# The gates of mixer 2 as rows: their weights become a stationary operand of 128 columns

## The reference, cut to what matters

```python
h = modulate(rms_norm_2(x, norm1_w), shift1, scale1)
p = h @ w_in                      # ..., last 16 columns are the gates
gates = p[..., o5:] + b_gates
...
gt = gates.astype(jnp.float32).reshape(B, S, 4, H).transpose(2, 0, 3, 1)
i_f, f_f, i_b, f_b = gt[0], gt[1], gt[2], gt[3]     # 4 kinds x 4 heads x 256 tokens
h_fwd = mlstm_chunkwise(q, k, v, i_f, f_f)
h_bwd = jnp.flip(mlstm_chunkwise(jnp.flip(q, 2), ..., jnp.flip(i_b, 2), jnp.flip(f_b, 2)), 2)
```

## Time and profile before

| | us |
|---|---|
| median of 3 runs | 2646.25 |
| lowest and highest of the 3 | 2640.28 and 2648.36 |
| the profiled execution, its own time | 2651.8 |
| its span in the profile | 2650.0 |
| PE busy | 2554.6 (96%) |
| DVE busy | 1435.3 (54%) |
| ACT busy | 1127.0 (43%) |
| POOL busy | 1222.3 (46%) |

### The profile page before, as it was taken

How to read it: one execution, slowest core, us unless ns; L and a number is a source line. 1 busy time by engine, 2 the same in 40 slices (tenths; PEclk the granted TensorE clock), 3 DMA queues, 4 the chain that set the end, 5 groups by cost and what they waited for, 6 DMA issues and landing times.

```text
span 2650.0 us, 48874 instructions
## 1 busy us (share of the span) xinstructions
PE 2554.6 (96%) x19040; PEld 2342.0 (88%) x19040; DVE 1435.3 (54%) x2359; ACT 1127.0 (43%) x1320; POOL 1222.3 (46%) x500
## 2 busy tenths in 40 slices
PE   7999999999899999999999999999999999999998
PEld 5887888889899999998888887789899999998886
DVE  3535242636667777776666434436566575444333
ACT  2252222443444444444444334443444444444443
POOL 2663333567444444444444364547344444444442
PEclk9999999999899999999999799999999999999999
DMA  9963343569577777776776464459566656555653
GB/s 397 391 243 127 132 187 156 226 241 347 210 275 271 267 266 269 269 272 249 286 261 258 142 270 158 153 198 344 192 222 219 245 214 222 183 189 176 196 186 125
DMA packets 140376, 611.85 MB, mean 231 GB/s; under 512 B 15584, under 2 KB 15968, under 8 KB 115680
## 3 DMA queue, kind: packets, MB, share of 16 engines
q1 hardware_dynamic: 140256, 610.14, 62.9%
HBM read 607.98 MB, written 2.10 MB: 230 GB/s over the span
## 4 chain that ended last, share of the span: by engine, by line
issue 46%; PE 31%; POOL 20%; DMA 1%; DVE 1%; POOLq 1%; ACT 0%; DVEq 0%; SPq 0%; ACTq 0%
PE psum L1905 31%; POOL wlo L1714 20%; DMA raw<-wstream 1%; DMA ada_raw<-adastream 0%; DVE xT L2227 0%; POOLq L1711 0%; POOLq L1713 0%; PE psum L2121 0%; ACT whi L1725 0%; DVE psum L2227 0%; DVE gslo L2219 0%; ACT arena L1728 0%; ACT gshi L1725 0%; DVE arena L2321 0%; POOLq L1714 0%
## 5 line engine op out<-in xcount | busy, mean ns | idle before, releaser
L1714 POOL TENSOR_TENSOR wlo<-raw,whi 128x1024 fp32r<-128x1024 f32 x496 | 1222.1, 2469 | 1398.9 <-ACT whi L1725 1398.4
L1905 PE MATMUL psum<-hi_h,whi 128*128 128x256 f32 x4224 | 1211.8, 287 | 15.0 <-issue 8.6
L1725 ACT ACTIVATE whi<-raw 128x1024 fp32r<-128x1024 f32 x760 | 800.6, 1059 | 998.2 <-PE psum L1905 785.9
L1905 PE MATMUL psum<-hi_h,wlo 128*128 128x256 f32 x4224 | 1196.6, 283 | 0.0
L1905 PE MATMUL psum<-lo_h,whi 128*128 128x256 f32 x4224 | 1196.0, 283 | 0.0
L1905 PEld LDWEIGHTS psum<-hi_h,whi 128*128 128x128 f32 x4224 | 805.4, 191 | 24.7 <-issue 13.9
L1905 PEld LDWEIGHTS psum<-hi_h,wlo 128*128 128x128 f32 x4224 | 805.3, 191 | 1.9 <-issue 1.7
L1905 PEld LDWEIGHTS psum<-lo_h,whi 128*128 128x128 f32 x4224 | 804.7, 191 | 0.0
L2219 DVE TENSOR_TENSOR wlo<-raw,whi 128x1024 fp32r<-128x1024 f32 x264 | 379.6, 1442 | 277.6 <-ACT whi L1725 277.6
L2227 DVE SCALAR_TENSOR_TENSOR psum<-ada_raw,cact,psum 128x256 f32<-128x256 f32 x702 | 287.5, 481 | 13.2 <-DMA ada_raw<-adastream 13.2
L1905 PE MATMUL psum<-whi,gshi 128*128 128x512 f32 x704 | 277.4, 394 | 4.0 <-DVE gslo L2219 3.5
(11 more groups left out here) (164 smaller groups left out, 1738.6 us busy)
## 6 DMA issues: line engine op xcount, KB each, us to landing
raw<-wstream SPq DMA_DIRECT2D x760, 512.0 KB, 4.6
ada_raw<-adastream SPq DMA_DIRECT2D x168, 1024.0 KB, 7.0
arena<-adastream SPq DMA_DIRECT2D x24, 1024.0 KB, 17.9
xT<-x_in SPq DMA_DIRECT2D x8, 512.0 KB, 7.0
y_out<-xT SPq DMA_DIRECT2D x4, 512.0 KB, 2.6
gs_pages<-tabs_in SPq DMA_DIRECT2D x2, 512.0 KB, 4.4
gs_pages<-rw_in SPq DMA_DIRECT2D x2, 512.0 KB, 7.8
tabs<-tabs_in SPq DMA_DIRECT2D x1, 738.0 KB, 9.5
```

What stands on the lines that cost most here:

```text
L1714: nc.gpsimd.tensor_tensor(wlo[:, q, :], raw[:, q, :], whi[:, q, :].bitcast(F32), ALU.subtract).then_inc(sem.lo_ready, 1)
L1725: return nc.scalar.activation(out_, in_, ACT.Copy, scale=scale)
L1905: return nc.tensor.matmul(o, lhsT, rhs, start=start, stop=stop, skip_group_check=True)
```

## The change

The 16 gate columns of each tile are spread over 128 columns, in groups of four at columns 0, 32, 64 and 96, with zeros between; the new buffer `wgs` (pages 4 to 7 of `arena`, free at that time) holds their high and low parts, 2 x 16 x 128 elements for each partition. DVE clears the whole buffer once (`wz0`), ACT writes the high parts and DVE the low parts into the groups. PE then takes the spread weights as the stationary operand and h as the moving one: 16 products of three matmuls with 256 columns, 48 matmuls in the place of 96. The gates come out as rows: input gates on partitions 0 to 63, forget gates on 64 to 127. The biases become one column for each partition, `gate_bias`, made by DVE with the identity. One matmul with a 64 x 64 identity moves the forget rows to partitions 0 to 63, in place of four. On DVE and ACT the operations on the gates now work on 256 elements in place of 16 or 32, and the two subtractions of `row_c` read the input gates from SBUF, where they read PSUM before. In ACT's program the copy of the gate weights waits for `wz0`; the call `ahead(0, 0)` ahead of it issues nothing new. The three clears of 256 elements become two and the one of 4096.

```diff
--- before.py
+++ after.py
@@ -363,6 +363,7 @@
         self.wg_hi = new("wg_hi")
         self.wg_ready = new("wg_ready")
         self.wz = new("wz")
+        self.wz0 = new("wz0")
         self.x_landed = new("x_landed")
         self.x_made = new("x_made")
         self.x_ready = new("x_ready")
@@ -419,7 +420,9 @@
         gain2, _ = sb("gain2", [P, 16])
         pc, _ = sb("pc", [P, 16])
         xT, _ = sb("xT", [P, KT, S])
-        arena, _ = sb("arena", [P, 15, 1024])
+        arena, arena_at = sb("arena", [P, 15, 1024])
+
+        wgs, _ = sb("wgs", [P, 2, KT, P], F32R, offset=arena_at + 4 * 4096)
         gT = arena[:, 0:11, :].rearrange("p a (b s) -> p (a b) s", s=S)
         gsf, _ = sb("gs_pages", [P, 4, 1024], F32, offset=gs_at)
 
@@ -1160,12 +1163,17 @@
 
             return 9 + ORDER2.index(name) + 1
 
-        wg_hi, wg_lo = gslo[:, 0, 0, :], gslo[:, 0, 1, :]
+
+        def gate_columns(part):
+            return wgs[:, part].rearrange("p k (g r) -> p k g r", r=32)[:, :, :, 0:4]
+
+        wg_in4 = small[:].rearrange("p (k g h) -> p k g h", g=4, h=4)
         dft = halves(19)
-        gate_tok = page(22)[:, 0:256].rearrange("p (k b c) -> p k b c", k=2, b=2)
-        gate_in = page(22)[:, 512:544].rearrange("p (b c) -> p b c", c=16)
-        f_min = page(22)[:, 544:560].rearrange("p (b c) -> p b c", c=8)
-        f_abs = page(22)[:, 560:576].rearrange("p (b c) -> p b c", c=8)
+        gate_bias = stat[:, 6:7]
+        gate_one = page(22)[:, 768:784]
+        FORGET = slice(64, 128)
+        gate_in = page(22)[:, 0:256]
+        f_min, f_abs = page(22)[FORGET, 256:512], page(22)[FORGET, 512:768]
         row_c, row_m, row_b, row_s = (tiles(14)[:, k, :] for k in range(4))
         FWD, BWD, BOTH = slice(0, 32), slice(32, 64), slice(0, 64)
         ccol = pc[:].rearrange("p (b r) -> p b r", r=8)
@@ -1179,7 +1187,7 @@
         hsq, hrms = page(13)[:, 0:512], page(13)[:, 512:768]
         mask_f, mask_b = page(20)[:, S:2 * S], page(20)[:, 0:S]
 
-        def pe_mix2(pe, st, mm, part, spot):
+        def pe_mix2(pe, st, mm, product, part, spot):
             def slot(g, s):
 
                 part(B2 + g * GS, g % 2, 2 * s, 2 * s + 2, "tok" if ORDER2[g][0] in "vu" else None,
@@ -1276,26 +1284,15 @@
                 slot(0, s)
 
             pe.wait_ge(sem.wg_ready, 1)
-            for tb in range(2):
-                o = bank[5][:, tb * 16:(tb + 1) * 16]
-                t = slice(tb * P, (tb + 1) * P)
-                for kt in range(KT):
-                    w = slice(kt * 16, kt * 16 + 16)
-                    mm(o, hhi[:, kt, t], wg_hi[:, w], tb == 0 and kt == 0, False)
-                    mm(o, hlo[:, kt, t], wg_hi[:, w], False, False)
-                    ins = mm(o, hhi[:, kt, t], wg_lo[:, w], False, kt == KT - 1)
-                    if tb and kt == KT - 1:
-                        ins.then_inc(sem.gates, 1)
+            for kt in range(KT):
+                ins = product(bank[5][:, 0:S], wgs[:, 0, kt, :], wgs[:, 1, kt, :], hhi[:, kt, :], hlo[:, kt, :],
+                              kt == 0, kt == KT - 1)
+            ins.then_inc(sem.gates, 1)
             slot(1, 0)
             slot(1, 1)
 
             pe.wait_ge(sem.gt_ready, 1)
-            for k in range(2):
-                for tb in range(2):
-                    ins = mm(bank[4][BOTH, k * S + tb * P:k * S + (tb + 1) * P], gate_tok[:, k, tb, :], ident,
-                       k == 0 and tb == 0, True)
-                    if k and tb:
-                        ins.then_inc(sem.rows_made, 1)
+            mm(bank[4][BOTH, 0:S], ident[FORGET, FORGET], f_min, True).then_inc(sem.rows_made, 1)
             slot(1, 2)
             slot(1, 3)
             slot(2, 0)
@@ -1383,9 +1380,11 @@
                 act.wait_ge(sem.dft_done, 3 * n + 3)
                 copy(halves(MF[n // 2])[:, n % 2, :], bank[6]).then_inc(sem.dft_out, 1)
 
+            ahead(0, 0)
             act.wait_ge(sem.tables2_landed, 48)
-            copy(wg_hi, small[:]).then_inc(sem.wg_hi, 1)
-            for s in range(4):
+            act.wait_ge(sem.wz0, 1)
+            copy(gate_columns(0), wg_in4).then_inc(sem.wg_hi, 1)
+            for s in range(1, 4):
                 ahead(0, s)
             kept("q")
             ahead(1, 0)
@@ -1447,31 +1446,33 @@
 
         def dve_mix2(dve, at, st, tt, ts, stt, unit_rows, scaled):
             V = nc.vector
-            dve.wait_ge(sem.wg_hi, 1)
-            tt(wg_lo, small[:], wg_hi.bitcast(F32), ALU.subtract).then_inc(*at.up(sem.wg_ready))
-            V.memset(page(22)[:, 0:256], 0.0).then_inc(*at.up(sem.step))
             V.memset(page(21)[:, 512:768], 1.0).then_inc(*at.up(sem.step))
             V.memset(page(21)[:, 768:1024], 0.0).then_inc(*at.up(sem.step))
+            dve.wait_ge(sem.slab_used, B2)
+            V.memset(wgs[:].bitcast(F32), 0.0).then_inc(*at.up(sem.wz0))
+            zeroed = at.last
+            tt(gate_one.rearrange("p (g h) -> p g h", h=4), ident.rearrange("p (g r) -> p g r", r=32)[:, :, 0:4],
+               col("bgates", 0, 16).rearrange("p (g h) -> p g h", h=4), ALU.mult).then_inc(*at.up(sem.step))
+            dve.wait_ge(*at.last)
+            V.tensor_reduce(gate_bias, gate_one, AX_X, ALU.add).then_inc(*at.up(sem.step))
+            dve.wait_ge(*zeroed)
+            dve.wait_ge(sem.wg_hi, 1)
+            tt(gate_columns(1), wg_in4, gate_columns(0).bitcast(F32), ALU.subtract).then_inc(*at.up(sem.wg_ready))
             unit_rows()
             one, zero = page(21)[BOTH, 512:768], page(21)[FWD, 768:1024]
 
             dve.wait_ge(sem.gates, 1)
-            tt(gate_in, bank[5][:, 0:32].rearrange("p (b c) -> p b c", c=16),
-               col("bgates", 0, 16).unsqueeze(1).broadcast_to([P, 2, 16]), ALU.add).then_inc(*at.up(sem.step))
-            dve.wait_ge(*at.last)
-            ts(f_min, gate_in[:, :, 8:16], 0.0, None, ALU.min).then_inc(*at.up(sem.step))
-            V.tensor_copy(gate_tok[:, 0].rearrange("p b (d x) -> p b d x", d=2)[:, :, :, 0:4],
-                               gate_in[:, :, 0:8].rearrange("p b (d x) -> p b d x", d=2)).then_inc(*at.up(sem.step))
-            dve.wait_ge(*at.last)
-            stt(f_abs, f_min, 2.0, gate_in[:, :, 8:16], ALU.mult, ALU.subtract).then_inc(*at.up(sem.f_abs))
+            ts(gate_in, bank[5][:, 0:S], gate_bias, None, ALU.add).then_inc(*at.up(sem.step))
+            dve.wait_ge(*at.last)
+            ts(f_min, gate_in[FORGET], 0.0, None, ALU.min).then_inc(*at.up(sem.step))
+            dve.wait_ge(*at.last)
+            stt(f_abs, f_min, 2.0, gate_in[FORGET], ALU.mult, ALU.subtract).then_inc(*at.up(sem.f_abs))
             dve.wait_ge(sem.f_ln, 1)
-            tt(gate_tok[:, 1].rearrange("p b (d x) -> p b d x", d=2)[:, :, :, 0:4],
-               f_min.rearrange("p b (d x) -> p b d x", d=2), f_abs.rearrange("p b (d x) -> p b d x", d=2),
-               ALU.subtract).then_inc(*at.up(sem.gt_ready))
+            tt(f_min, f_min, f_abs, ALU.subtract).then_inc(*at.up(sem.gt_ready))
             unit_rows()
 
             dve.wait_ge(sem.rows_made, 1)
-            gi, gf = bank[4][:, 0:S], bank[4][:, S:2 * S]
+            gi, gf = gate_in, bank[4][:, 0:S]
             V.tensor_tensor_scan(row_b[BOTH], one, gf[BOTH], 0.0, ALU.mult, ALU.add).then_inc(*at.up(sem.step))
             dve.wait_ge(*at.last)
             tt(row_b[BWD], row_b[BWD], gf[BWD], ALU.subtract).then_inc(*at.up(sem.step))
@@ -2203,7 +2204,7 @@
             down(B1_DOWN, 0, 2, 4, True)
             st["free"] = {0: (sem.x_ready, 8), 1: (sem.x_ready, 8)}
             st.update(unit=MIX_UNITS2[0], units=MIX_UNITS2, spots=SPOTS2, slabs=0, after_taken={MIX_UNITS2[0]: 10})
-            pe_mix2(pe, st, mm, part, spot)
+            pe_mix2(pe, st, mm, product, part, spot)
             output(B2_OUT, MIX2, 4, 12, (sem.mix_split, 4, 2))
             up(B2_UP, 1, 24, [(8, 1), (3, 0)])
             down(B2_DOWN, 1, 5, 16, False)
```

## The result

The changed kernel takes 2628.65 us (median of 5 runs, 2623.95 to 2629.92), the kernel before 2643.34 us in the same comparison (5 runs). The ratio is 0.9941 with a 95% interval of 0.9928 to 0.9955: 15.6 us less, between 11.9 and 19.0. The forecast was 13.3 us less, 2633.0 us.

The account below looks back on a forecast made before the run. PE was taken as the bound, busy 2554.6 of 2650.0 us. The terms 11.0 + 1.8 + 0.5 = 13.3 us, taken from the median 2646.25 us, gave 2633.0 us, range 2627 to 2640.

Parts of the forecast that it names:

- The product: Gate product on PE: 48 matmuls of 256 columns at 0.120 us replace 96 of 16 columns, 11.0 us less.
- Rival E: Gate product: PE's time goes by moving columns, so the new product costs 5.0 us more, 2651.3 us; chance 0.01.
- The slab behind it: Slab after the gate product: clock doesn't fall, so its first 20 matmuls take 2.4 us, not 4.2; 1.8 us less.
- Rival B: Gate product and slab behind: the clock falls all the same, only 7.1 us less, 2639.2 us; chance 0.02.
- The turn: Turn of gates to rows on PE: one matmul in place of four, 0.5 us less.
- The weights: Gate weights behind DVE's long clear: ready at 1498.5 to 1499.4, before PE comes at 1499.92; cost 0 us.
- rival A: Before the gate product: POOL holds up DVE's clear and subtraction, weights late, PE stands 3.3 us, 2636.3 us; chance 0.10.
- What was queued behind ACT's wait: High parts of slabs 9 to 11 and SP's slabs 13 to 15 come later, but before PE wants them; cost 0.
- the gates' chain: DVE and ACT operations on the gates grow to 256 elements, done at 1513.6 before PE's turn at 1519.2; cost 0.
- the stream: SP's load of modulation weights waits for PE's spot at the end of slab 11, so everything behind moves with PE.
- Rival C: Behind the spot: transfers are the limit, PE comes earlier only to wait, time about 2646 us; chance 0.05.
- Rival D: DVE's clear of 4096 elements takes 26.8 us, PE stands 21.7 us, 2657.5 us, longer than before; chance 0.02.

Follow-up runs that it names:

- the wide product: The kernel before, each of its 96 gate matmuls moving 128 columns (spread weights) in place of 16, h stationary as before: 2636.19 us, ratio 0.9982.
- the doubled products: Gate product computed twice over, in the kernel before (2665.42 us, ratio 1.0082) and in the changed kernel (2635.84 us, ratio 0.9967).
- clear_twice: The changed kernel with DVE's clear of 4096 elements done twice: 2633.97 us, ratio 0.9964.
- before_again: The kernel before, measured once more with no edit: 2643.70 us against 2643.06 us, ratio 1.0002.
- before_twice: The kernel before with its gate product computed twice over (192 matmuls of 16 columns): 2665.42 us, ratio 1.0082.

## Why the prediction was right, and where it was off

**The product, 11.0 us.** Right: 16.78 to 5.80 us, 10.98 us. That the count of matmuls and not their moving columns sets the time is shown by 0.109, 0.111 and 0.120 us for 16, 128 and 256 columns. Rival E, the time by moving columns, is refuted by the wide product. By the figures of "TensorE: Matmul & The Clock Gate", section "Back-to-back issue gap", of the Trainium skill, the 96 narrow matmuls would have taken 2.4 us; but that section gives them for an isolated matmul, and has it that in a stream of weight loads and matmuls both set the spacing, which the prediction left out. The same page of the Trainium skill has the price that held, in "LDWEIGHTS (loading the stationary operand)": the number of columns divided by 1.2, in ns, so 107 ns for 128. The trace agrees, with 109 ns. That the weight load is what takes this time rests on this agreement: no run multiplied twice with the same weights.

**The slab behind it, 1.8 us.** Right: 1.91 us. Its reason, that the narrow matmuls bring the clock down, was an inference from one place in one trace; the wide and the doubled products bear it out. Rival B didn't occur in any of the seven profiles that have 256 columns and no long standstill.

**The turn, 0.5 us.** Right: 0.45 us.

**The weights, 0 us with a margin of 0.5 to 1.4 us.** Half right, and the one step that failed: that DVE is free for this part at a fixed time. Two things were off. First, the clear of 4096 elements was sized 3.5 us, by the slope between two rows. It takes 4.27 us, if the idle time that stands ahead of each long clear is counted with it, 0.80 us here and 0.2 us ahead of the clear of 1024 elements (0.9 + 0.2 = 1.1 us, again 1.04 to 1.07 ns an element). I take this idle time as the start of the clear, which the row leaves out. The second clear of clear_twice, which ends 4.4 us after the first, fits that. My other end, sixteen times the short one, was the nearer one, and with it the margin was right: 0.7 us where DVE was free in time. "VectorE: DVE Perf Modes", section "Zero memsets can be issued as uint32 (trn2)", of the Trainium skill has a clear at one cycle for each element, which at the 0.96 GHz of that page is 4.27 us, an estimate; the measured 4.27 us agree. The 0.3 us from ACT's copy to DVE's subtraction were misread too, without harm: DVE's operation before had begun only at 1493.26, and in the changed kernel the subtraction began 0.1 us after the copy. Second, I took DVE's start of this part as fixed (1493.27 in a trace where PE came at 1499.92). It isn't: when the last two subtractions of the norm each meet a low part of POOL, DVE is free 20.8 us after slab 0 began, and otherwise 18.7 us. In the three profiles with the narrow product (before, before_again, before_twice) it was the latter; in the changed kernel both occur. So the wait is 1.56 us in two of three profiles of the changed kernel and 0 in one. It is rival A in a milder form, by another mechanism than the one I named: not the clear was held up by POOL, but the subtractions ahead of it.

**What was queued behind ACT's wait, the gates' chain, the stream.** All cost nothing, as forecast. POOL made the low parts of slabs 9 to 11 from 1499.45 on, slab 8 ran without a gap, and the load of modulation weights came at 1517.52 in place of 1531.32, 13.8 us earlier. Rival C is refuted by the table: the heads take no longer than before. Rival D didn't come: the clear ran at 1.04 ns an element.

**The sum.** 13.3 us were forecast; the medians differ by 14.7, and the three comparisons of the changed kernel give 0.9941, 0.9946 and 0.9935, thus 14 to 17 us. Locally it is 13.4 us without the wait and 11.8 us with it. What is over, some 3 us, is no more than the half-width of the intervals (some 3.5 us). It agrees in size with the 5 us of low clock that the runs have less of outside this stretch, and with the shorter heads, but that isn't shown to be an effect of the change. So the closeness of 13.3 to 14.7 is in part luck: a wait that was forecast at nothing took 1.5 us in two profiles of three, and some 3 us came from elsewhere. The time itself came out 4.4 us below 2633.0, of which 2.9 us are the baseline, 2646.25 us for three runs and 2643.34 us for five.

## What to carry to other kernels

A product of few moving columns, with new weights for each matmul, cost 0.109 us a matmul here, as much as with eight times the columns, and it brought the clock to half, for most of itself and for the start of what came next. So make the small matrix the stationary operand, if need be padded with zeros to 128 columns, and stream the large one. Work that such a layout needs (a clear, a copy) belongs where its engine is idle, and behind what that engine must deliver first; look in the trace for operations of its neighbours that get longer beside it. And read a single profile's total with care: here one stretch differed by 5.8 us between two executions of the same code (149.95 and 144.16 us), so cut several traces at the same points before looking for a cause, and before ruling one out.

## What the runs showed of the hardware that I had not expected

- With PE busy for 100% of a window in the profile, matmuls of 16 columns, 0.109 us apart, had the granted clock down to 0.50 after 3.8 us and kept it there for 33 us; matmuls of 128 columns, 0.111 us apart, kept it at 1.00.
- DVE's clear of 4096 elements has 3.47 us in its row and 0.80 us of idle ahead of it, in each profile that has it behind a short clear. POOL's clear of the same size has a row of 3.51 us, with no idle time ahead of it when it stood behind other work; DVE's four residual operations beside it took 1.66 us, as without it.
- DVE's operation on 2 elements, with one input and its output in SBUF, took 2.29 us beside POOL's subtractions and 0.17 us without them. "SBUF — State Buffer", section "Who interferes with whom", of the Trainium skill names this kind of operation among those that can take both ports and so contend with POOL; the rows agree.
- Idle time of PE of 3.61 us was followed by a low clock in the product behind it (7.33 us in place of 5.7), idle time of 1.56 us was not.
